# A decoder layer's SwiGLU on one core: the down product also by seven products, in phases of 1024 tokens

## The reference

```
x1 = x + gate1 * (merged @ w_out)
h2 = rms_norm(x1, norm2_g) * (1.0 + scale2) + shift2
ff = (silu(h2 @ w_gate) * (h2 @ w_up)) @ w_down      # w_gate, w_up (1024, 2816), w_down (2816, 1024)
y  = x1 + gate2 * ff
```

## Time and profile before

| | |
|---|---|
| time, median of 3 executions | 2693.78 us (2693.47 to 2693.97) |
| the profiled execution | 2692.48 us, of which the span 2690.7 us |
| mean granted TensorE clock in it | 0.988 of full speed |
| PE busy / PEld busy | 97% / 84% |
| DVE busy / ACT busy / POOL busy | 70% / 48% / 14% |
| DMA | 473.93 MB, 176 GB/s over the span |

### The profile page before, as it was taken

One profiled execution on the slowest core, in us unless ns is written; L12 is line 12 of the kernel. 1 busy time (PEld: TensorE's weight loads), 2 busy tenths in 40 slices (PEclk: granted clock), 3 DMA queues, 4 the chain that ended last, 5 costly groups with the idle time before them and its releaser, 6 DMA issues.

```text
span 2690.7 us, 46777 instructions
## 1 busy us (share of the span) xinstructions
PE 2618.1 (97%) x18021; PEld 2251.1 (84%) x18021; DVE 1887.0 (70%) x3500; ACT 1290.2 (48%) x2508; POOL 373.6 (14%) x535
## 2 busy tenths in 40 slices
PE   6999999999999999999899999999999999999998
PEld 3678888777787778778899989999899998999976
DVE  6647887557767558677888568885687867787644
ACT  4212221337889556665555444554445544455432
POOL 2107787430001000000000000000000000000000
PEclk8999999999999989999999999999999999999999
DMA  9663334853333896443855646656456564565521
GB/s 336 199 201 114 120 120 141 282 182 121 123 121 110 338 354 208 154 158 120 264 169 173 219 128 185 181 157 230 131 178 180 168 212 144 169 175 159 168 94 58
DMA packets 340183, 473.93 MB, mean 176 GB/s; under 512 B 31553, under 2 KB 252993, under 8 KB 331378
## 3 DMA queue, kind: packets, MB, share of 16 engines
q1 hardware_dynamic: 320968, 353.78, 40.9%
q0 software_dynamic: 16544, 116.29, 13.0%
q10 hardware_dynamic: 2450, 0.87, 0.1%
HBM read 390.09 MB, written 147.37 MB: 200 GB/s over the span
## 4 chain that ended last, share of the span: by engine, by line
PE 72%; ACT 3%; DVE 2%; issue 1%; DMA 0%; ACTq 0%; SPq 0%; DVEq 0%
PE f_ps L2728 31%; PE f_ps L2749 18%; PE c_ps_w L2165 7%; PE a_o_ps L406 2%; PE a_s_ps L377 2%; PE a_t_ps L388 2%; PE c_ps_glu L2140 2%; PE b_ps_t L1787 1%; ACT a_probs L444 1%; PE a_o_ps L414 1%; PE b_ps_s L1799 1%; PE b_ps_o L1824 1%; PE a_t_ps L357 1%; PE b_ps_p L1809 1%; PE c_ps_mT L2149 0%
## 5 line engine op out<-in xcount | busy, mean ns | idle before, releaser
L2728 PE MATMUL f_ps<-f_x,f_ws 128*128 128x256 f32 (+1 forms) x7392 | 894.8, 284 | 13.1 <-ACT f_us L2856 6.4
L2728 PEld LDWEIGHTS f_ps<-f_x,f_ws 128*128 128x128 f32 x7392 | 893.5, 189 | 14.4 <-issue 10.3
L2749 PE MATMUL f_ps<-f_ws,f_ws 128*128 128x512 f32 x2112 | 483.5, 390 | 0.0
L2749 PEld LDWEIGHTS f_ps<-f_ws,f_ws 128*128 128x128 f32 x2112 | 395.7, 188 | 91.9 <-issue 8.4
L946 PE MATMUL p_out_ps<-p_w,p_hT 128*128 128x512 f32 x1620 | 379.8, 392 | 1.1 <-DVE p_qk L1222 1.1
L946 PEld LDWEIGHTS p_out_ps<-p_w,p_hT 128*128 128x128 f32 x1620 | 300.9, 188 | 73.0 <-issue 11.6
L2910 DVE TENSOR_TENSOR f_ws<-f_raw,f_ws 128x1024 fp32r<-128x1024 f32 x176 | 215.1, 1222 | 189.6 <-ACT f_ws L2841 187.7
L2910 DVE TENSOR_TENSOR f_ws<-raw,f_ws 128x1024 fp32r<-128x1024 f32 x176 | 215.0, 1222 | 181.6 <-ACT f_ws L2841 179.6
L2841 ACT ACTIVATE f_ws<-f_raw 128x1024 fp32r<-128x1024 f32 x176 | 185.8, 1057 | 242.2 <-PE f_ps L2749 139.3
L2841 ACT ACTIVATE f_ws<-raw 128x1024 fp32r<-128x1024 f32 x176 | 185.8, 1057 | 236.2 <-PE f_ps L2749 134.3
L444 ACT ACTIVATE a_probs<-a_probs,a_o 128x256 f32<-128x256 f32 (+1 forms) x384 | 171.1, 451 | 1.6 <-DVE a_o L487 1.6
(11 more groups left out here) (375 smaller groups left out, 3702.7 us busy)
## 6 DMA issues: line engine op xcount, KB each, us to landing
out_dram<-in_cache_k_dram POOLq DMA_DIRECT2D x8, 4088.0 KB, 14.4
out_dram<-in_cache_v_dram POOLq DMA_DIRECT2D x8, 4088.0 KB, 14.4
raw<-in_w_gate_dram SPq DMA_DIRECT2D x88, 256.0 KB, 4.1
raw<-in_w_up_dram SPq DMA_DIRECT2D x88, 256.0 KB, 4.6
f_raw<-in_w_gate_dram SPq DMA_DIRECT2D x88, 256.0 KB, 4.1
f_raw<-in_w_up_dram SPq DMA_DIRECT2D x88, 256.0 KB, 4.6
f_raw<-in_w_down_dram SPq DMA_DIRECT2D x88, 256.0 KB, 3.1
raw<-in_w_down_dram SPq DMA_DIRECT2D x88, 256.0 KB, 3.2
```

Of the source, the lines that this page charges most:

```text
L2728: mm = pe.matmul(ps[place % 8][:, 0:w], ws[s % SLOTS][:, y, j * 512 + k * 128:j * 512 + (k + 1) * 128], x_half(b, p, z)[:, k], start=(p < ...
L2749: mm = pe.matmul(ps[down_bank(b, h, j)][:, :], ws[(s + 1) % SLOTS][:, y, at + j * 128:at + (j + 1) * 128], ws[s % SLOTS][:, z, at:at + 512 ...
```

## The change

The down product is computed with seven products too. For that its activations must be 2 x 2 quarters (even and odd row groups of w_down's 22, and two halves of the tokens) of a large block: two gate-and-up blocks (1024 tokens) are now one round (`ROUNDS = 2`), with one down phase at its end.

- **Activations.** `multiply` writes four quarters into a stage buffer, DVE makes the sums (`stage_sums`: four operations of 128 x 256 per pair), and SP stores the seven factors of a pair to DRAM (`store_sums`, 896 KB), from where the down phase loads them.
- **Weights of down.** In round 0 POOL loads w_down by 1 MB, makes the four sums of quarters (`t_sum`: four operations of 128 x 512 for each of 11 row pairs) and stores them to DRAM (`t_step`, one step per pair).
- **Down phase.** 77 pieces (7 products x 11 row pairs) per round. A piece is one slot: 512 columns of an activation factor and 512 of a weight factor, one load of 256 KB each, split by one `fill_hi` and one `fill_lo`; it takes 4 x 3 matmuls of 512 columns. Over both rounds that is 2 x 77 x 12 = 1848 matmuls. After products 0, 3 and 4 ACT copies four A banks out (`down_copy`), and DVE reads four tiles for each of the four outputs (`read_y`, `gated_y`, `summed_y`).
- **Inputs of the odd blocks.** There is no down phase before blocks 1 and 3. Their inputs go to a buffer of their own (`f_xn`) during the even block; POOL makes their four sums (`xn_sum`, 128 x 1024, at pairs 6 to 9), and ACT and DVE split them (`x_hi`, `x_lo`) in the last pair of the even block, one per product.
- **Sample rows.** They go with block 2. Their down product is 44 narrow matmuls in block 3, four after product 3 of each pair, from unsplit w_down that POOL loads by 1 MB a pair (`load_quarters`) after the cache copy of that pair.
- **PSUM banks** follow tables (`BANKS_G`, `BANKS_D`); the last tiles of the output go out after the last product instead of tile by tile.

```diff
-        for b in range(FB):
-            load_rows(b, 0)
-            for i in range(4):
-                pool.wait_ge(product, 4 * (b * NPAIRS + (1, 4, 6, 9)[i]))
-                move(4 * b + i)
...
+        for b in range(FB):
+            r = b // 2
+            for n in range(NPAIRS):
+                g = b * NPAIRS + n
+                if g:
+                    pool.wait_ge(product, 4 * g)
+                if n in (1, 4, 6, 9):
+                    move(4 * b + (1, 4, 6, 9).index(n))
+                if r == 0:
+                    t_step(g)
+                if b == SAMPLE_BLOCK + 1:
+                    if n:
+                        pool.wait_ge(in_parts, n)
+                    else:
+                        pool.wait_ge(d_y[Y_BUF[C12]], 64)
+                    load_quarters(n)
+                if b % 2 == 0 and 6 <= n < 10:
+                    xn_sum(b + 1, n - 6)
...
+        def t_sum(i):
+            out, left, right = ((0, 1, 0), (1, 3, 1), (3, 3, 0), (2, 2, 3))[i]
+            return pool.tensor_tensor(wq[:, out, :], wq[:, left, :], wq[:, right, :], ALU.subtract).then_inc(t_summed, 1)
+
+        def t_step(i):
+            k = i // 2
+            if i % 2 == 0:
+                if k:
+                    pool.wait_ge(wq_moved, 32 * k)
+                load_quarters(k)
+            else:
+                pool.wait_ge(wq_moved, 32 * k + 16)
+                t_sum(0)
+                pool.wait_ge(t_summed, 4 * k + 1)
+                t_sum(1)
+                t_sum(2)
+                pool.wait_ge(t_summed, 4 * k + 3)
+                t_sum(3)
...
+        def sample_parts(n):
+            if n == 0:
+                bank_ready("sample")
+                pe.wait_ge(product, 4 * (SAMPLE_BLOCK + 1) * NPAIRS)
+            pe.wait_ge(wq_moved, 32 * DEPTH + 16 * (n + 1))
+            for h in range(2):
+                for x in range(2):
+                    c = 2 * h + x
+                    mm = pe.matmul(ps[SAMPLE_BANK][32 * c:32 * c + NS, :], a_s[:, 2 * n + x, :], wq[:, 2 * x + h, :], start=(n == 0), stop=(n == DEPTH - 1))
             mm.then_inc(in_parts, 1)
...
+        def down_group(r, p, ks):
...
+                for k in ks:
+                    slot = ws[(first + k) % SLOTS]
+                    for x, (y, z) in enumerate(((0, 0), (0, 1), (1, 0))):
+                        mm = pe.matmul(ps[bank][:, :], slot[:, y, j * 128:(j + 1) * 128], slot[:, z, 512:1024],
+                                       start=(p < 3 and k == 0 and x == 0), stop=(k == DEPTH - 1 and x == 2), skip_group_check=p > 2)
...
+                    if b == SAMPLE_BLOCK + 1 and p == 3:
+                        sample_parts(n)
...
+        def stage_sums(g):
+            at = lambda i: stage[g % 2][:, i, :]
+            dve.wait_ge(product, 4 * g + 4)
+            dve.tensor_tensor(at(2), at(6), at(5), ALU.add).then_inc(staged, 1)
+            sub(at(4), at(0), at(6)).then_inc(staged, 1)
+            dve.wait_ge(staged, 4 * g + 1)
+            sub(at(3), at(2), at(0)).then_inc(staged, 1)
+            dve.wait_ge(staged, 4 * g + 3)
+            sub(at(6), at(1), at(3)).then_inc(staged, 1)
...
+                        if p == 1 and pair:
+                            stage_sums(b * NPAIRS + n - 1)
+                        if b % 2 == 0 and n == NPAIRS - 1:
+                            x_lo(b + 1, p)
...
+            for j in range(4):
+                read_y(ROUNDS - 1, C12, j)
+                gated_y(ROUNDS - 1, C12, j)
+                summed_y(ROUNDS - 1, C12, j)
```

More of the change, by code:

```diff
@@ L2454 @@
 FB = 4
-HALVES_W = (256, 256, 256, 256 + NS // 2)
+SAMPLE_BLOCK = 2
+HALVES_W = tuple(256 + (NS // 2 if b == SAMPLE_BLOCK else 0) for b in range(FB))
 HALF_W = max(HALVES_W)
@@ new lines, in pool_part @@
+            if b % 2 == 0:
+                continue
+            sums_stored(pool, (b + 1) * NPAIRS)
+            if r:
+                pool.wait_ge(d_y[Y_BUF[C11]], 64 * r)
+            y_dma(r, C11, False)
+            if r == 0:
+                pool.wait_ge(wq_moved, 32 * DEPTH)
+            else:
+                pool.wait_ge(in_parts, DEPTH)
+            y_dma(r, C22, False)
+            for c, after in ((C11, C21), (C22, C12), (C21, None), (C12, None)):
+                if r == ROUNDS - 1 and c == C12:
+                    break
+                pool.wait_ge(added, y_added(r, c, 3))
+                y_dma(r, c, True)
+                if after is not None:
+                    pool.wait_ge(d_y[Y_BUF[c]], 64 * r + 32)
+                    y_dma(r, after, False)
@@ L2720, in multiplied @@
             if p < 3:
-                bank_ready(place)
+                bank_ready("pair", b, n, role, j)
             elif p < 6:
```

680 lines of the change are left out of this document (376 added, 304 removed).

## The result

The kernel after takes 2732.19 us (median of 4, 2728.36 to 2734.65), the kernel before 2693.62 in the same session: a ratio of 1.0143 with an interval from 1.0125 to 1.016. It is slower by 38.6 us, not by 12.9, and lies just outside the range. The sign is as forecast, and most of the terms came out near their size.

A forecast was written before the change was run, and what follows sets the result against it. The prediction took PE's matmuls, busy 97% of the span, as the bound. Its terms, -68.0 + 3.9 - 2.0 + 54 + 15 + 9 + 1, made +12.9 us on 2693.8: 2707 us, range 2658 to 2732.

The forecast's parts named there:

- term 7: Down phases: loads run eight pieces ahead, block 2's inputs go ahead of them once; +1 us (0 to 10).
- term 4: Block 3, pairs 1, 4, 6, 9: PE waits for sample rows' w_down load behind the cache copy, clock drops; +54 us.
- terms 5 and 6: Gate and up: POOL's sums hold DVE back in round 0, +15 us; DVE's splits of odd blocks' inputs, +9 us.
- Term 1: Down phases: fewer matmuls, 1848 at 0.2267 us each; -68.0 us.
- Term 2: The tail after PE's end: the last four tiles' dependent operations end 5.4 us after PE, now 1.5; +3.9 us.
- term 3: Starts of blocks 1 and 3: PE's idle moments there go; -2.0 us.
- Rival A: Block 3: the w_down load lands in time, so its +54 us falls away; 2653 us, chance 0.17.
- Rival C: Round 0: DVE becomes the bound and its lateness never drains; +41 us, 2735 us, chance 0.08.
- Rival D: Block 0: weights land late in fuller DMA traffic, one to two stalls of 10 us; 2722 us, chance 0.07.

## Why the prediction was wrong in size

**What failed: term 7, "+1 us", and two terms that were missing.** Term 7 reads "The inputs of block 2 (7 x 512 KB) go ahead of them once" and puts a price on the transfers. The price was in the issues. Block 2 takes the sample columns too, so its seven parts are 14 DMAs. SP spent 19 us on them, about as long as the eight pieces last that are loaded ahead. Round 0 lost 9.9 us against the forecast. Spreading the loads gave all of it back (220.4 to 209.5 us). Round 1 lost 4.2, of which 2.2 are PE's idle time behind DVE's wait for `f_ys` (the rest is in no row that I read):

```profile
DVE f_tmps L3179 <- DMA f_ys<-scratch_x: 9.5, 1, 9.5
```

One missing term is the start, +3.9: the change put the input loads into two groups, and the first product then waits for four loads when it needs one. Separate semaphores gave the idle time back. The other is the clock behind the waits of blocks 0 and 1, which term 4 priced for its own waits and terms 5 and 6 put at nothing; it is below.

**Term 1** was right: 816 matmuls in 185.24 us are 0.2270 each, against 0.2267. **Term 2** was 1.2 us too high, **term 3** showed no error that the table could separate.

**Term 4** was right in place, cause and size: 44.6 us of waits and 7.1 us of slower matmuls make 51.7 against 54 (the clock costs 1.8 us a wait, not 2.5), and moving the load ahead of the copy took 47 us from blocks 2 and 3. Rival A falls: the load issued at 2249.41 lets PE go at 2267.12, 17.7 us later and some 4 us after its copy's 14.4 us, though the same load lands 5.6 us after its issue in the median of block 3. No run separates the 2 us that the sum took off as a fixed part. The DMA issues of blocks 2 and 3 answer to the earlier trace rows:

```profile
out_dram<-in_cache_v_dram POOLq DMA_DIRECT2D x8, 4088.0 KB, 14.4
...
out_dram<-scratch_v_new POOLq DMA_DIRECT2D x8, 8.0 KB, 14.9
```

**Terms 5 and 6** forecast 22 us of waits in blocks 0 and 1, and they were 21.1: 1.10, 1.14 and 0.66 in pairs 1, 3 and 5, 3.76 and 3.69 in pairs 7 and 9 (3.4 forecast), 1.1 to 1.5 four times in block 1, and 1.46 and 4.30 for the splits of block 1's inputs (1 and 6 forecast). What was left out is the clock behind them: 41.48 us for 336 matmuls instead of 40.00, 21.61 for 168 instead of 20.11, 81.53 for 672 instead of 80.0, and in the first pair 7.64 for 48 instead of 5.88 and 28.03 for 216 instead of 25.7. In the 6.2 us behind the wait of 3.76 the granted clock is 0.72 of full speed, so part of them ran at the lower level of 1.2 GHz; behind the wait of 1.14 it is 1.00, the full 2.4 GHz. That is some 8 us in all, the gap to +27.9. And the cause was half of the truth, so the match in size is partly luck: with the copies moved away POOL's sums and the splits alone made 14.9 us of waits. Taking POOL's sums away was worth nothing, because the stores of `f_stage` behind the 4 MB copies were as late. Rival C (DVE becomes the bound) gave 2735 us, near the time measured, but by chance: it asked for 52 us of waits in these blocks and for several us in nearly every pair, and they were 21.1, with three of the eleven waits over 2 us. Rival D had late transfers, but of weights in block 0, and it was the stores that DVE waited for.

The sum then is 12.9 + 3.9 + 9.9 + 4.2 + 7.2 + 2.2 (block 3's and 2's remainder) - 1.2 = 39.1 us, for 39.4 between the profiled spans and 38.6 between the medians.
